# More gate projections by seven products, and stick-breaking attention started two blocks of input projection earlier, in another order of its blocks

## The chip, the cores and the metric

One Trainium2 chip, one of its cores. The metric is the device time of one execution of the whole program in microseconds (us), as the median of several executions.

## What is computed

Two transformer layers on 1024 positions of width 1024, all in float32. The first layer projects the normed input with `w_in` and feeds four branches (a short convolution, stick-breaking attention, an RWKV-7 recurrence, a gated spatial mix), weights each by its own sigmoid gate (4 x 1024 columns of the same projection), sums them, and ends in a feed-forward network. The second layer has two kinds of softmax attention. The parts that the change touches:

```
def short_conv_mixer(z, conv_w):
    b_gate, c_gate, xin = jnp.split(z, 3, axis=-1)
    return b_gate * causal_dwconv(c_gate * xin, conv_w)

def stick_breaking_attention(q, k, v):
    """A[t,s] = sig(z_ts) * prod_{s<j<t} (1 - sig(z_tj)), s < t."""
    ...
    def block(args):
        qi, bi = args
        z = jnp.einsum('bhqd,bhkd->bhqk', qi, kh).astype(jnp.float32) * scale
        mask = kpos[None, :] < qpos[:, None]
        log_beta = jax.nn.log_sigmoid(z)
        log_keep = jnp.where(mask, log_beta - z, 0.0)
        suffix = lax.cumsum(log_keep, axis=3, reverse=True) - log_keep
        attn = jnp.where(mask, jnp.exp(log_beta + suffix), 0.0)
        return jnp.einsum('bhqk,bhkd->bhqd', attn.astype(vh.dtype), vh)
...
gates = jax.nn.sigmoid((proj[..., GATE_OFF:] + gate_b)).reshape(bsz, t, N_BRANCH, D_MODEL)
merged = (gates[:, :, 0] * (y_a @ sc_out) + gates[:, :, 1] * (y_b @ sb_out)
          + gates[:, :, 2] * (y_c @ rw_out) + gates[:, :, 3] * (y_d @ sg_out))
```

## The kernel before

**Blocks.** The input projection is cut into blocks of 128 output columns by all 1024 positions. To keep float32 precision each operand is split into a high and a low part, and a product takes three matmuls (high by high, low by high, high by low). A block is 8 slices of the inner dimension x 2 halves of 512 positions x 3 = 48 matmuls of 128x512 (`whole`, L1244 to L1246, and `dense`, L1372 to L1374, which is the same in four quarters of 12). Results land in one of two places of PSUM, `gp[:, t % 2]`, where t is the block's number; whoever reads the block out adds one to `p_free0` or `p_free1`, and block t+2 waits for that. POOL splits the raw weights of each block (`split_weights`: a cast to `w_hi`, L954, and a subtraction to `w_lo`, L956). Which columns a block takes is given by the tuple `DENSE`.

**Order on TensorE.** Eight blocks (t = 0 to 7); then pairs of gate blocks (`gate_product`, L1403 to L1405), each pair by seven products of 12 matmuls in place of the eight that two plain blocks take; the sums between the products are DVE's (L2723 to L2735), the sigmoids ACT's. Then blocks t = 8 to 13 (v, q and k of the attention); then blocks 14 to 27 (`T_SB` = 14 to `T_RW` = 28) with the stick-breaking attention between their quarters; then the eight blocks of the recurrence, and all the rest.

**Stick-breaking attention in steps.** A *unit* m of the sixteen is one block of 128 queries (`qb`) for one pair of heads (`ft`); its scores are `w` = 128 (qb + 1) columns wide for each of the two heads. Before the change unit m is `qb, ft = divmod(m, 2)`. A *step* is one quarter of a block (12 matmuls) and then what `sb_pieces(step)` names, in this order: outputs, turns, scores.

- scores (PE, L1445), up to 512 columns a step, so units 8 to 15 need two steps; ACT makes both sigmoids from them (`sb_sig`, L2210; `sb_keep`, L2211);
- the cut of the diagonal (POOL `sb_cut`, L1001), once for the unit; in POOL's program it stands among the `split_weights` calls, which stand at `step % 4 == 2`;
- two running products (DVE scans, L2767), then the multiplication of `sb_sig` by them (L2772);
- turns (PE transposes, L1456), up to four tiles a step, each copied to `sb_pt` by ACT (L2227) before the next turn may write the same bank;
- outputs (PE, L1466) a step after their turn; when a unit's last one is done, ACT copies `y_b` (L2223), and the next unit's first output waits for that (`sb_y_free`).

Unit m starts its scores at step `SB_START[m]`. Its first turn is at step `SB_START[m + 1]`, and waits for DVE (`sb_p`); an engine takes its work in program order, so the matmuls behind that turn wait with it. There are 56 steps.

**Short convolution.** Blocks 14 to 17 are the convolution's output gate (columns 0, 1; ACT copies them to `y_a`) and its input gate (2, 3; ACT copies to `sc_c`); blocks 18 and 19 are its input. DVE reads these from PSUM in `short_conv` after units 8 and 9, and multiplies with `y_a` at its end (L2759). Blocks 20 to 27 are gates; ACT puts their sigmoids into `gate_late`, which lies where `sc_c` was, so it waits for `sc_done` first.

## Time and profile before

| | |
|---|---|
| median of 3 runs | 2448.02 us (2446.23 to 2448.09) |
| the profiled execution | 2444.71 us, span 2443.0 us |
| PE busy in the span | 2372.1 us (97%) |
| weight loads (PEld) | 1881.1 us (77%) |
| DVE, ACT, POOL busy | 1169.0 (48%), 769.2 (31%), 1112.4 us (46%) |
| DMA queue q1, share of 16 engines | 24.5% |
| blocks 14 to 27 with the attention between | 388.8 to 623.0 us of the span |

The span is the time from the profile's first to its last instruction, and the execution's own time is 1.7 us more. PE is busy nearly all the time, so what matters is how many matmuls it has, and the stretches in which it is idle. The profiled execution was 3.3 us below the median of the runs.

### The profile page before, as it was taken

How to read it: one execution, taken by the hardware profiler on the slowest of the kernel's cores; microseconds unless marked ns; L12 is line 12 of the kernel's file. 1: busy time of each engine (PE TensorE's matmuls, PEld its weight loads, DVE VectorE, ACT ScalarE, POOL GpSimd, SP SyncE). 2: the span in 40 equal slices, each digit the busy share in tenths (PEclk: the TensorE clock that was granted, in tenths of full speed). 3: DMA queues.
4: the chain of work that ended last, by engine and by line, in shares of the span. 5: the costliest groups of instructions: out<-in, count | busy, mean ns of one | idle time of the engine just before them, and what ended most of it. 6: DMA issues, size and time to landing. Idle time of an engine off the chain costs nothing.

```text
span 2443.0 us, 36336 instructions
## 1 busy us (share of the span) xinstructions
PE 2372.1 (97%) x15494; PEld 1881.1 (77%) x15494; DVE 1169.0 (48%) x1445; ACT 769.2 (31%) x1191; POOL 1112.4 (46%) x755
## 2 busy tenths in 40 slices
PE   7999999999999999999999999999999999999999
PEld 6888887666779868878888887888777886656677
DVE  7811101554195355676667775333443216755621
ACT  4233312333222121254434441011332006564511
POOL 4477733333234278577777773343732220013221
PEclk9999999999999999999999999999999999999999
DMA  5233321011200146422222225322213112000024
GB/s 198 79 104 104 104 77 43 27 52 59 63 27 13 38 155 207 138 69 90 83 87 78 78 95 190 104 86 69 52 43 104 49 37 63 13 12 24 2 64 126
DMA packets 208250, 189.83 MB, mean 78 GB/s; under 512 B 16714, under 2 KB 186929, under 8 KB 207834
## 3 DMA queue, kind: packets, MB, share of 16 engines
q1 hardware_dynamic: 208090, 187.51, 24.5%
q8 instruction: 123, 2.02, 0.3%
q14 instruction: 37, 0.30, 0.0%
HBM read 141.31 MB, written 45.13 MB: 76 GB/s over the span
## 4 chain that ended last, share of the span: by engine, by line
PE 81%; issue 7%; DVE 6%; POOL 5%; ACT 2%; DMA 0%; SPq 0%; POOLq 0%; DVEq 0%; ACTq 0%
PE gp L1244 8%; PE gp L1246 8%; PE gp L1245 8%; PE sm L1785 3%; PE sm L1786 3%; PE sm L1784 3%; PE gp L1784 3%; PE gp L1785 3%; PE gp L1786 3%; PE gp L1887 3%; PE gp L1903 2%; POOL w_lo L956 2%; PE sm L1813 2%; PE sm L1815 2%; PE sm L1814 2%
## 5 line engine op out<-in xcount | busy, mean ns | idle before, releaser
L954 POOL CAST w_hi<-w_raw 128x1024 fp32r<-128x1024 f32 (+1 forms) x101 | 110.1, 1090 | 730.8 <-PE gp L1246 364.4
L956 POOL TENSOR_TENSOR w_lo<-w_raw,w_hi 128x1024 fp32r<-128x1024 f32 (+1 forms) x109 | 295.8, 2713 | 8.7 <-ACT w_hi L2314 0.5
L1244 PE MATMUL gp<-h_hi,w_hi 128*128 128x512 f32 x704 | 282.5, 401 | 0.0
L1246 PE MATMUL gp<-h_hi,w_lo 128*128 128x512 f32 x704 | 274.3, 390 | 0.0
L1245 PE MATMUL gp<-h_lo,w_hi 128*128 128x512 f32 x704 | 273.9, 389 | 0.0
L1244 PEld LDWEIGHTS gp<-h_hi,w_hi 128*128 128x128 f32 x704 | 132.2, 188 | 33.1 <-issue 6.6
L1245 PEld LDWEIGHTS gp<-h_lo,w_hi 128*128 128x128 f32 x704 | 132.2, 188 | 31.0 <-issue 4.3
L1246 PEld LDWEIGHTS gp<-h_hi,w_lo 128*128 128x128 f32 x704 | 132.1, 188 | 28.0
L2767 DVE TENSOR_TENSOR_SCAN sb_run<-sb_keep,ones_row 128x128 f32<-128x128 f32 (+7 forms) x32 | 77.2, 2453 | 135.7 <-POOL sb_keep L1001 135.7
L1161 POOL TENSOR_TENSOR w_lo<-w_sum,w_hi 128x512 fp32r<-128x512 f32 x66 | 96.3, 1459 | 45.8 <-ACT w_hi L2373 45.8
L2534 ACT ACTIVATE att_s<-att_s,small 128x1024 f32<-128x1024 f32 (+7 forms) x128 | 99.0, 775 | 5.2 <-DVE small L3242 4.8
L1372 PE MATMUL gp<-h_hi,w_hi 128*128 128x512 f32 x240 | 99.3, 414 | 0.0
L1374 PE MATMUL gp<-h_hi,w_lo 128*128 128x512 f32 x240 | 93.9, 391 | 0.0
L1373 PE MATMUL gp<-h_lo,w_hi 128*128 128x512 f32 x240 | 93.8, 391 | 0.0
L2546 ACT COPY att_pt<-gp 128x512 f32<-128x512 f32 (+1 forms) x80 | 44.9, 562 | 120.3 <-PE gp L1887 120.3
L1887 PE MATMUL gp<-ident,att_s 128*128 128x128 f32 x576 | 77.5, 280 | 0.0
L2456 ACT CAST g_hi<-g_stage 128x1024 fp32r<-128x1024 f32 x22 | 23.1, 1054 | 168.2 <-DMA g_stage<-g_spill 123.7
L1784 PE MATMUL gp<-x_hi_T,w_hi 128*128 128x512 f32 x176 | 69.8, 396 | 5.9 <-DVE up_u L3086 5.2
L1113 POOL TENSOR_TENSOR merged<-merged,gated 128x1024 f32<-128x1024 f32 x24 | 64.8, 2700 | 17.8 <-DVE gated L2958 15.4
L1813 PE MATMUL gp<-g_hi,w_hi 128*128 128x512 f32 x176 | 69.2, 393 | 3.0 <-DVE g_lo L3131 3.0
L1887 PEld LDWEIGHTS gp<-ident,att_s 128*128 128x128 f32 x576 | 61.6, 141 | 12.0 <-issue 10.1
L1001 POOL TENSOR_SCALAR_AFFINE_SELECT sb_sig<-sb_sig 128x256 f32<-128x256 f32 x16 | 6.5, 408 | 140.2 <-ACT sb_keep L2211 140.2
(631 smaller groups left out, 6296.2 us busy)
## 6 DMA issues: line engine op xcount, KB each, us to landing
w_raw<-in_w_in SPq DMA_DIRECT2D x69, 512.0 KB, 4.0
gate_in<-gates_spill SPq DMA_DIRECT2D x30, 512.0 KB, 4.4
gates_spill<-gate_out SPq DMA_DIRECT2D x24, 512.0 KB, 5.9
w_raw<-in_w_up SPq DMA_DIRECT2D x22, 512.0 KB, 5.2
up_raw<-in_w_up SPq DMA_DIRECT2D x22, 512.0 KB, 5.1
g_spill<-hid SPq DMA_DIRECT2D x22, 512.0 KB, 2.6
g_stage<-g_spill SPq DMA_DIRECT2D x22, 512.0 KB, 4.3
w_raw<-in_w_down SPq DMA_DIRECT2D x22, 512.0 KB, 3.6
```

What stands on the lines that cost most here:

```text
L954: pool.tensor_copy(w_hi[:, t % 2, 0:n], w_raw[:, t % 2, 0:n]).then_inc(s["w_high"], 1)
L956: pool.tensor_tensor(w_lo[:, t % 2, 0:n], w_raw[:, t % 2, 0:n], w_hi[:, t % 2, 0:n].bitcast(F32), ALU.subtract).then_inc(s["w_split"], 1)
L1244: pe.matmul(o, wh, hi[:, k0 + k, c], start=(k == 0), stop=False)
L1245: pe.matmul(o, wh, lo[:, low[k] if low else k0 + k, c], start=False, stop=False)
L1246: mm = pe.matmul(o, wl, hi[:, k0 + k, c], start=False, stop=(k == n - 1))
L1372: pe.matmul(o, wh, h_hi[:, k, c], start=(k == 0), stop=False)
L1784: pe.matmul(o, wh, xh[:, :], start=(i < 4 and j == 0), stop=False, skip_group_check=True)
L1785: pe.matmul(o, wh, xl[:, :], start=False, stop=False, skip_group_check=True)
L1786: mm = pe.matmul(o, wl, xh[:, :], start=False, stop=(j == 3), skip_group_check=True)
L1813: pe.matmul(o, wh, hi[:, cols], start=(k == 0), stop=False)
L1887: mm = pe.transpose(bank(4 + r % 3)[:, P * n:P * n + P], s_buf[:, at_place(u), hh, P * k:P * k + P], ident[:, :])
L2534: act.activation(s_buf[:, at_place(u), hh, 0:w], s_buf[:, at_place(u), hh, 0:w], ACT.Exp, scale=-1.0, bias=at_small(0, u, hh), accum_out=a ...
```

## The change

Two more pairs of gate blocks are made by seven products (12 pairs in place of 10), and four fewer plain gate blocks (4 in place of 8) are left at the end of the attention's stretch. The plain blocks ahead of the attention are v, v, q0, k0; blocks 12 and 13 (q1, k1) now stand inside the attention's stretch, which is blocks 12 to 23: 12 blocks, 48 steps. So the attention begins at the fifth of the blocks behind the pairs. Units are taken in a new order, `SB_ROWS`: query blocks 0 to 3 of the first pair of heads, then 0 to 3 of the second, then as before. `SB_START` is closer, and a unit's first turn is at `SB_START[m + 1] + 1`, one step later than the next unit's first scores. Before the scores of unit 4, the first with q1 and k1, PE waits until both have been read out. The convolution's input gate is blocks 14 and 15, its input 16 and 17, its output gate 18 and 19: ACT copies the last no more, and DVE multiplies the block in PSUM with `sc_c` into `y_a` (`conv_gated`, after units 12 and 13). DVE's scans wait for `sb_p`, its own last multiplication.

```diff
 T_PAIRS = 8
-T_SB = 14
-T_RW = 28
+T_SB = 12
+T_RW = 24
...
-GATE_PAIRS = 10
-DENSE = (20, 22, 23, 21) + (24, 25, 26, 27) + (10, 11, 6, 7, 8, 9) + (0, 1, 2, 3, 4, 5) + tuple(range(48, 56))
-GATES = (0, 1, 2, 3) + tuple(4 + GATE_PAIRS * m + p for p in range(GATE_PAIRS) for m in (1, 0)) + tuple(range(24, 32))
+GATE_PAIRS = 12
+DENSE = (20, 22, 23, 21) + (24, 25, 26, 27) + (10, 11, 6, 8, 7, 9) + (2, 3, 4, 5, 0, 1) + tuple(range(52, 56))
+GATES = (0, 1, 2, 3) + tuple(4 + GATE_PAIRS * m + p for p in range(GATE_PAIRS) for m in (1, 0)) + tuple(range(28, 32))
 RW_ORDER = (6, 2, 0, 4, 3, 1, 5, 7)
 BRANCH_GATES = (0, 3, 1, 2)
-SB_START = tuple(2 + 2 * m for m in range(8)) + tuple(18 + 4 * m for m in range(9))
+SB_ROWS = ((0, 0), (1, 0), (2, 0), (3, 0), (0, 1), (1, 1), (2, 1), (3, 1)) + tuple((n // 2, n % 2) for n in range(8, 16))
+SB_START = (0, 2, 4, 6, 8, 9, 10, 12, 14, 17, 20, 23, 26, 30, 34, 38, 42)
...
             starts = [(m, step - SB_START[m]) for m in range(PAIRS)]
-            turns = [(m, step - SB_START[m + 1]) for m in range(PAIRS)]
-            return ([(m, c - 1) for m, c in turns if 1 <= c <= m // 4 + 1],
-                    [(m, c) for m, c in turns if 0 <= c <= m // 4],
-                    [(m, c) for m, c in starts if 0 <= c <= m // 8])
+            turns = [(m, step - SB_START[m + 1] - 1) for m in range(PAIRS)]
+            return ([(m, c - 1) for m, c in turns if 1 <= c <= sb_turns(m)],
+                    [(m, c) for m, c in turns if 0 <= c < sb_turns(m)],
+                    [(m, c) for m, c in starts if 0 <= c < sb_parts(m)])
...
                         for z in range(2):
                             pe.wait_ge(s[f"p_free{z}"], frees_before(T_SB + z))
+                    elif (m, c) == (4, 0):
+                        for z in range(2):
+                            pe.wait_ge(s[f"p_free{z}"], frees_before(T_SB + 2 + z))
                     sb_scores(m, c)
...
                 n = DENSE[t]
-                if n in (4, 5):
+                if n < 2 or n in (4, 5):
...
-                elif n < 2:
-                    act.copy(y_a[:, n, :], ps).then_inc(done, 1)
...
-                for z in range(2):
-                    dve.wait_ge(s[f"p_free{z}"], frees_before(T_SB + 4 + z))
+                dve.wait_ge(s[f"p_free{n}"], frees_before(t))
...
-                ins = dve.tensor_tensor(y_a[:, n, :], y_a[:, n, :], acc, ALU.mult)
+
+            def conv_gated(n):
+
+                t = T_SB + 6 + n
+                dve.wait_ge(s["p_ready"], t + 1)
+                dve.tensor_tensor(y_a[:, n, :], gp[:, t % 2, :], sc_c[:, n, :], ALU.mult).then_inc(s[f"p_free{t % 2}"], 1)
                 if n == 1:
-                    ins.then_inc(s["sc_done"], 1)
+                    for z in range(2):
+                        dve.wait_ge(s[f"p_free{z}"], frees_before(t) + 1)
+                    dve.tensor_copy(small[:, 8:9], ones[:, 0:1]).then_inc(s["sc_done"], 1)
 
             for m in range(PAIRS):
-                w = P * (m // 2 + 1)
+                w = P * (SB_ROWS[m][0] + 1)
                 wait("sb_cut")
+                if m:
+                    dve.wait_ge(s["sb_p"], m)
...
-                if m in (8, 9):
-                    short_conv(m - 8)
+                if m in (9, 10):
+                    short_conv(m - 9)
+                elif m in (12, 13):
+                    conv_gated(m - 12)
```

What this does to the order of instructions is read from the two programs. "waits" names the semaphores that an instruction waits for.

On POOL, around the cuts of the units 9 to 11 in the program after (`L1010` is the cut, `L963` and `L965` the split of a block's weights; these rows begin with the cut of unit 9):

```order
L1010 AFFINE_SELECT sb_sig<-sb_sig 128x2x128 [waits sb_e]
L1010 AFFINE_SELECT sb_keep<-sb_keep 128x2x128
L1010 AFFINE_SELECT sb_sig<-sb_sig 128x2x128 [waits sb_e]
L1010 AFFINE_SELECT sb_keep<-sb_keep 128x2x128
L963 CAST w_hi<-w_raw 128x1024 [waits p_ready,w_loaded0]
L965 TENSOR_TENSOR w_lo<-w_raw,w_hi 128x1024 [waits w_high]
L1010 AFFINE_SELECT sb_sig<-sb_sig 128x2x128 [waits sb_e]
L1010 AFFINE_SELECT sb_keep<-sb_keep 128x2x128
L963 CAST w_hi<-w_raw 128x1024 [waits p_ready,w_loaded1]
L965 TENSOR_TENSOR w_lo<-w_raw,w_hi 128x1024 [waits w_high]
```

Before, from unit 8 on, each unit's cut was followed by a split; the rows begin with the cut of unit 8 (`L1001`, splits `L954` and `L956`):

```order
L1001 AFFINE_SELECT sb_sig<-sb_sig 128x2x128 [waits sb_e]
L1001 AFFINE_SELECT sb_keep<-sb_keep 128x2x128
L954 CAST w_hi<-w_raw 128x1024 [waits p_ready,w_loaded0]
L956 TENSOR_TENSOR w_lo<-w_raw,w_hi 128x1024 [waits w_high]
L1001 AFFINE_SELECT sb_sig<-sb_sig 128x2x128 [waits sb_e]
L1001 AFFINE_SELECT sb_keep<-sb_keep 128x2x128
```

The cuts of units 9 and 10 now stand together, with no split between them, and the split behind the cut of unit 10 is that of block 18.

On PE, the whole of step 10's attention work in the program after (`L1475` an output, `L1465` a turn, `L1454` scores, then the next quarter's first matmul):

```order
L1475 MATMUL sm<-sb_pt,v_sb 64x128 [waits sb_pt_copied,sb_y_free]
L1475 MATMUL sm<-sb_pt,v_sb 64x128 x3
L1465 MATMUL sm<-ident,sb_sig 128x128 [waits sb_pt_copied]
L1465 MATMUL sm<-ident,sb_sig 128x128 x3
L1465 MATMUL sm<-ident,sb_sig 128x128 [waits sb_pt_copied,sb_p]
L1465 MATMUL sm<-ident,sb_sig 128x128
L1454 MATMUL sm<-k_sb,q_sb 128x384 [waits sb_e] x2
L1381 MATMUL gp<-h_hi,w_hi 128x512
```

No step before had two turns, each with its own wait for ACT's copy; here unit 3's second turn and unit 4's first stand one behind the other.

On DVE, from the scans of unit 12 to the first of unit 14 after the change (`L2786` a scan, `L2791` the multiplication, `L2774` `conv_gated`):

```order
L2786 SCALAR_TENSOR_TENSOR sb_run<-sb_keep,ones_row 128x896 [waits sb_p,sb_cut]
L2786 SCALAR_TENSOR_TENSOR sb_run<-sb_keep,ones_row 128x896
L2791 TENSOR_TENSOR sb_sig<-sb_sig,sb_run 128x2x895 [waits sb_run]
L2774 TENSOR_TENSOR y_a<-gp,sc_c 128x1024 [waits p_ready]
L2786 SCALAR_TENSOR_TENSOR sb_run<-sb_keep,ones_row 128x896 [waits sb_p,sb_cut]
L2786 SCALAR_TENSOR_TENSOR sb_run<-sb_keep,ones_row 128x896
L2791 TENSOR_TENSOR sb_sig<-sb_sig,sb_run 128x2x895 [waits sb_run]
L2774 TENSOR_TENSOR y_a<-gp,sc_c 128x1024 [waits p_ready]
L2778 COPY small<-ones 128x1 [waits p_free1,p_free0]
L2786 SCALAR_TENSOR_TENSOR sb_run<-sb_keep,ones_row 128x1024 [waits sb_p,sb_cut]
```

Before, the two blocks of the output gate were read out by ACT at once, and DVE's part of it was the last row of each `short_conv`, behind units 8 and 9:

```order
L2756 SCALAR_TENSOR_TENSOR sc_c<-sc_cx,col,sc_c 128x1023 [waits dve_own]
L2756 SCALAR_TENSOR_TENSOR sc_c<-sc_cx,col,sc_c 128x1022 [waits dve_own]
L2759 TENSOR_TENSOR y_a<-y_a,sc_c 128x1024 [waits dve_own]
L2767 SCALAR_TENSOR_TENSOR sb_run<-sb_keep,ones_row 128x640 [waits sb_cut]
L2767 SCALAR_TENSOR_TENSOR sb_run<-sb_keep,ones_row 128x640
L2772 TENSOR_TENSOR sb_sig<-sb_sig,sb_run 128x2x639 [waits sb_run]
```

The read-out of blocks 18 and 19 now stands on DVE behind the scans of units 12 and 13.

## Rows read from the trace of the kernel before

**Rows 1.** Busy time by stretch: us; busy us and instructions of each engine; granted clock.

```profile
388.80:623.00 234.20, 224.66 (x1202) 159.19 (x1201) 110.35 (x59) 77.63 (x164) 72.93 (x60) 1.00 0.15 46
623.00:800.00 177.00, 167.19 (x2727) 141.48 (x2727) 102.43 (x94) 47.21 (x51) 63.10 (x33) 0.99 0.13 38
...
730.00:740.00 10.00, 9.38 (x300) 9.15 (x302) 5.88 (x7) 2.19 (x3) 4.69 (x2) 0.83 0.01 3
```

**Rows 2.** Waits from 388 to 624: who waited for whom, us, times, longest.

```profile
PEld sm L1456 <- DVE sb_sig L2772: 12.7, 10, 2.4
...
PE sm L1456 <- DVE sb_sig L2772: 9.5, 8, 2.2
```

**Rows 3.** Timeline of ACT, read-out of two plain blocks: start, duration, [idle before].

```profile
378.01 1.02 ACT L2132 COPY k_sb<-gp 128x1024 f32<-128x1024 f32 x1 [9.85 <-PE gp L1246]
388.89 1.02 ACT L2132 COPY k_sb<-gp 128x1024 f32<-128x1024 f32 x1 [9.86 <-PE gp L1246]
```

**Rows 4.** Timeline of DVE, the same sum in two pairs of gate blocks.

```profile
158.69 0.69 DVE L2723 TENSOR_TENSOR ones_row<-ones_row,sm 128x512 f32<-128x512 f32 x1 [7.52 <-PE sm L1405]
...
177.73 0.69 DVE L2723 TENSOR_TENSOR ones_row<-ones_row,gp 128x512 f32<-128x512 f32 x1 [7.52 <-PE gp L1405]
```

**Rows 5.** Timeline of PE, unit 15 from last scores to first turn.

```profile
590.40 1.13 PE L1445 MATMUL sm<-k_sb,q_sb 64*128 64x512 f32 x4
...
594.40 0.66 PE L1466 MATMUL sm<-sb_pt,v_sb 128*64 128x128 f32 x8
...
598.34 0.66 PE L1466 MATMUL sm<-sb_pt,v_sb 128*64 128x128 f32 x8
...
602.28 0.66 PE L1466 MATMUL sm<-sb_pt,v_sb 128*64 128x128 f32 x8
604.30 0.66 PE L1456 MATMUL sm<-ident,sb_sig 128*128 128x128 f32 x4 [1.36 <-DVE sb_sig L2772]
```

**Rows 6.** Timeline of ACT, first sigmoid of those scores.

```profile
591.56 0.60 ACT L2210 ACTIVATE sb_sig<-sm 128x512 f32<-128x512 f32 x1 [0.47 <-PE sm L1445]
```

**Rows 7.** Timeline of POOL: cut of unit 15, split behind it, a later undisturbed split.

```profile
593.70 0.41 POOL L1001 TENSOR_SCALAR_AFFINE_SELECT sb_sig<-sb_sig 128x256 f32<-128x256 f32 x1 [13.61 <-ACT sb_keep L2211]
...
594.41 1.04 POOL L954 CAST w_hi<-w_raw 128x1024 fp32r<-128x1024 f32 x1
595.54 4.24 POOL L956 TENSOR_TENSOR w_lo<-w_raw,w_hi 128x1024 fp32r<-128x1024 f32 x1
...
608.97 2.40 POOL L956 TENSOR_TENSOR w_lo<-w_raw,w_hi 128x1024 fp32r<-128x1024 f32 x1
```

**Rows 8.** Timeline of DVE: scans of units 6, 7 and 15, multiplication of unit 15.

```profile
447.86 2.34 DVE L2767 TENSOR_TENSOR_SCAN sb_run<-sb_keep,ones_row 128x512 f32<-128x512 f32 x2 [4.80 <-POOL sb_keep L1001]
...
456.53 5.30 DVE L2767 TENSOR_TENSOR_SCAN sb_run<-sb_keep,ones_row 128x512 f32<-128x512 f32 x2 [5.07 <-POOL sb_keep L1001]
...
594.50 7.42 DVE L2767 TENSOR_TENSOR_SCAN sb_run<-sb_keep,ones_row 128x1024 f32<-128x1024 f32 x2 [9.94 <-POOL sb_keep L1001]
601.95 2.29 DVE L2772 TENSOR_TENSOR sb_sig<-sb_sig,sb_run 128x2046 f32<-128x2046 f32 x1
```

**Rows 9.** Timeline of PE and DVE: last scores, next output, multiplication of unit 9 (640 columns).

```profile
484.37 0.49 PE L1445 MATMUL sm<-k_sb,q_sb 64*128 64x128 f32 x4
...
487.74 0.66 PE L1466 MATMUL sm<-sb_pt,v_sb 128*64 128x128 f32 x8
...
492.50 1.49 DVE L2772 TENSOR_TENSOR sb_sig<-sb_sig,sb_run 128x1278 f32<-128x1278 f32 x1
```

**Rows 10.** Timeline of PE and ACT: an output and its copy, a turn and its copy.

```profile
441.31 0.44 PE L1466 MATMUL sm<-sb_pt,v_sb 128*64 128x128 f32 x4
443.11 0.66 PE L1456 MATMUL sm<-ident,sb_sig 128*128 128x128 f32 x4 [1.36 <-DVE sb_sig L2772]
...
441.80 0.27 ACT L2223 COPY y_b<-sm 128x128 f32<-128x128 f32 x1 [2.76 <-PE sm L1466]
443.81 0.59 ACT L2227 COPY sb_pt<-sm 128x512 f32<-128x512 f32 x1 [1.74 <-PE sm L1456]
```

More of the change, by code:

```diff
@@ L56 @@
 T_PAIRS = 8
-T_SB = 14
-T_RW = 28
-T_BR = 36
-T_WO = 44
-T_FFN = 52
+T_SB = 12
+T_RW = 24
+T_BR = 32
+T_WO = 40
+T_FFN = 48
 T_IN2 = T_FFN + FT
@@ L66 @@
 T_END = T_OUT + 8
-P_RW = 28
-P_BR = 36
+P_RW = 24
+P_BR = 32
 P_WO = P_BR + 32
@@ L579, in hybrid_layers, with sb_turns, sb_parts @@
         PAIRS = 2 * NB
+        def sb_turns(m):
+            return SB_ROWS[m][0] // 2 + 1
+        def sb_parts(m):
+            return SB_ROWS[m][0] // 4 + 1
         def sb_chunks(m):
-            before = sum(n // 4 + 1 for n in range(m))
-            return [(c, before + c) for c in range(m // 4 + 1)]
+            before = sum(sb_turns(n) for n in range(m))
+            return [(c, before + c) for c in range(sb_turns(m))]
         def sb_blocks(m, c):
-            return [2 * k + hh for k in range(2 * c, min(2 * c + 2, m // 2 + 1)) for hh in range(2)]
+            return [2 * k + hh for k in range(2 * c, min(2 * c + 2, SB_ROWS[m][0] + 1)) for hh in range(2)]
         def sb_pieces(step):
             starts = [(m, step - SB_START[m]) for m in range(PAIRS)]
-            turns = [(m, step - SB_START[m + 1]) for m in range(PAIRS)]
-            return ([(m, c - 1) for m, c in turns if 1 <= c <= m // 4 + 1],
-                    [(m, c) for m, c in turns if 0 <= c <= m // 4],
-                    [(m, c) for m, c in starts if 0 <= c <= m // 8])
+            turns = [(m, step - SB_START[m + 1] - 1) for m in range(PAIRS)]
+            return ([(m, c - 1) for m, c in turns if 1 <= c <= sb_turns(m)],
+                    [(m, c) for m, c in turns if 0 <= c < sb_turns(m)],
+                    [(m, c) for m, c in starts if 0 <= c < sb_parts(m)])
         def sb_scores_through(m, c):
-            return sum(2 * (n // 8 + 1) for n in range(m)) + 2 * (c + 1)
+            return sum(2 * sb_parts(n) for n in range(m)) + 2 * (c + 1)
         def at_unit(u):
@@ L754, in _ @@
                 load_weights(t + 2)
-                if t >= T_SB + 6:
-                    store_dense(t, t + 4, gate_late)
+                if t >= T_SB + 8:
+                    store_dense(t, t + 8, gate_late)
             for t in range(T_RW + 2, T_BR + 2):
@@ L996, in sb_cut @@
             def sb_cut(m):
-                pool.wait_ge(s["sb_e"], sb_scores_through(m, m // 8))
-                qb = m // 2
+                pool.wait_ge(s["sb_e"], sb_scores_through(m, sb_parts(m) - 1))
+                qb = SB_ROWS[m][0]
                 for buf, fill in ((sb_sig[:, m % 2], 0.0), (sb_keep, 1.0)):
@@ L1049, in _ @@
                     for m, c in sb_pieces(step)[2]:
-                        if c == m // 8:
+                        if c == sb_parts(m) - 1:
                             sb_cut(m)
@@ L1437, in sb_scores @@
             def sb_scores(m, c):
-                qb, ft = divmod(m, 2)
+                qb, ft = SB_ROWS[m]
                 w = P * (qb + 1)
@@ L1459, in sb_output @@
             def sb_output(m, c, r):
-                qb, ft = divmod(m, 2)
+                qb, ft = SB_ROWS[m]
                 if c == 0 and m:
@@ L1467, in sb_output @@
                                    sb_pt[:, b, :], start=(k == 0), stop=(k == qb), skip_group_check=True)
-                if c == m // 4:
+                if c == sb_turns(m) - 1:
                     mm.then_inc(s["sb_y"], 1)
@@ L2114, in dense_out @@
                 if n >= 24:
-                    q = t - 4 if t < T_PAIRS else t + 4
+                    q = t - 4 if t < T_PAIRS else t + 8
                     if q >= 2:
@@ L2202, in sb_sigmoids @@
             def sb_sigmoids(m, c):
-                w = min(HALF, P * (m // 2 + 1) - HALF * c)
+                w = min(HALF, P * (SB_ROWS[m][0] + 1) - HALF * c)
                 if c == 0 and m:
@@ L2215, in _ @@
                 if step % 4 == 3:
-                    if step == 4 * 6 + 3:
+                    if T_SB + step // 4 == T_SB + 8:
                         act.wait_ge(s["sc_done"], 1)
@@ L2220, in _ @@
                 for m, c in outputs:
-                    if c == m // 4:
+                    if c == sb_turns(m) - 1:
                         wait("sb_y")
-                        act.copy(y_b[:, m % 2, P * (m // 2):P * (m // 2) + P], sm[:, 3, 0:P]).then_inc(s["sb_y_free"], 1)
+                        qb, ft = SB_ROWS[m]
+                        act.copy(y_b[:, ft, P * qb:P * qb + P], sm[:, 3, 0:P]).then_inc(s["sb_y_free"], 1)
                 for m, c in turns:
```

## Prediction

> **What bounds the kernel now.** Read first, in the profile's page, the busy shares: TensorE is busy 97% of the span, so only two things can move the time, the number of matmul slots and the stretches in which PE is idle. Then the busy time by stretch. Blocks 14 to 27 with the attention between take 234.2 us of which PE is busy 224.7 [rows 1]; the reader is to see that 9.5 us are idle, in a stretch where DVE is busy only 110 us and ACT and POOL less than 80. No engine is full there, so something is late rather than too much. The waits of the stretch say what: all of PE's 9.5 us, 8 times, are turns that wait for DVE's multiplication; the weight-load queue in front of the same turns shows 12.7 us, 10 times [rows 2]. The timelines then give the chain from a unit's last scores to its first turn.
>
> **A matmul slot.** Two plain blocks in a row are read out 10.88 us apart [rows 3], for 48 matmuls, so a quarter is 2.72 us and a matmul 0.227. The same sum in two successive gate pairs is 19.04 us apart [rows 4], for 84 matmuls: again 0.227, so the pairs run without a gap.
>
> **Term 1, the pairs.** Two pairs more cost 2 x 19.04 = 38.08 us of PE; four plain blocks less give 4 x 10.88 = 43.52. The difference is 5.44 us, 24 matmuls. It lies on the path, since PE is the path in both stages. What the pairs add on ACT, DVE and POOL lies beside PE, which has not waited for them in the ten pairs there were; the four blocks' splits and stores are gone. The attention's own work on PE is the same 40 turns, 40 outputs and 24 pieces of scores, only in another order, so it costs nothing more. ACT's two copies to `y_a` and the last row of DVE's `short_conv` are replaced by one DVE multiplication each; all of this lies beside PE.
>
> **Term 2, the turns that wait.** Take unit 15. From its last scores on PE to the first turn that could start is 604.30 - 590.40 = 13.9 us [rows 5]: 1.16 to the first sigmoid [rows 6], 2.1 for four sigmoids, 0.8 for the cut [rows 7], 7.42 for two scans and 2.29 for the multiplication [rows 8]. What PE has to do in that time, its *cover*, is counted in steps. Scores and a quarter are 594.40 - 590.40 = 4.00, so 1.28 for scores of 512 columns; a step of output, turn and quarter is 3.94 [rows 5], so 1.22 for output and turn together and 0.6 for one of them. Before, `SB_START[15]` is 46, so the last scores are at step 47 and the turn at step 50: 1.28 + 3 x 2.72 + 2 x 1.22 + 0.6 = 12.5 us against 13.9. The missing 1.4 us is the wait that the row shows, 1.36. This arithmetic can now be done for the new numbers.
>
> After, the last scores of unit 15 are at step 39 and its turn at step 43: 1.28 + 4 x 2.72 + 3 x 1.22 + 0.6 = 16.4 us against the same 13.9, as one more quarter and one more output and turn lie between. That is 2.5 us to spare. Units 12 to 14 have the same four quarters, and the next unit's first scores too, so 3 or more. Narrower units have shorter chains. Unit 9 (640 columns) took 493.99 - 484.37 = 9.6 us, and its last scores (128 columns) 487.74 - 484.37 - 2.72 = 0.65 of PE [rows 9]. After, unit 8 has 3 quarters: 0.65 + 8.16 + 1.22 + 0.6 + 1.28 = 11.9 us, 2.3 to spare. For 768 columns I interpolate between 9.6 and 13.9: 11.1. The cover of units 10 and 11 is 12.8 and 13.2 (last scores 0.85, 3 quarters, one or two steps of output and turn, scores of the next unit, an output): 1.7 and 2.1 to spare. For 512 columns, four widths of 128 less than 1024 at 0.8 each (scans 0.53: (7.42 - 5.30) / 4; multiplication 0.27), the chain is 10.7 [rows 8]; unit 7 has 12.7 of cover, 2.0 to spare. Units 0 to 6 come out at 2 or more. So no turn waits for DVE; before, ten did.
>
> What was lost: PE's idle time says 9.5, the load queue 12.7 [rows 2]. A matmul's record (0.39 on the page) is longer than its slot (0.227), so a wait behind a quarter hides 0.16 or more of itself; half of them stand there. I take 10.5, with 9.5 and 12.7 as ends.
>
> **What makes a chain longer.** A scan that meets a split is slower: two scans of 512 columns took 2.34 us alone and 5.30 beside the split that stands behind the cut of unit 7, 2.96 more [rows 8]; the split's subtraction took 4.24 in place of 2.40 [rows 7]. The chain of 13.9 has this in it. In the new order of POOL, splits stand behind the cuts of units 0, 2, 5, 7, 8 and 10 to 15, behind 11 units in place of 12, and I have counted every chain above with it.
>
> The other side of it is the split itself. That of block 18 now stands behind the cut of unit 10, late, as the block starts two quarters further on. From unit 10's last scores: 3.0 to the end of the cut, 4.8 for a split beside two scans of 768 (1.13 and 3.7, between 2.40 and 4.24), 7.8 in all; the cover is 0.85 + 2 x 2.72 + 1.22 + 2.3 = 9.8. It costs nothing, with 2 us to spare. The Trainium skill (SBUF — State Buffer, section "Who interferes with whom") says that VectorE and GpSimd share a port pair under an exclusive lock, and that the loser waits out the winner's whole instruction. That the trace agrees is seen in the two rows of scans: they are slowed, and so is the split. By that rule the subtraction could lose both scans of 768, 1.7 us each, in place of the 1.3 that the rows give it; block 18 would start 0.1 us late, and the sum below would be 14.0 in place of 14.1.
>
> **Term 3, a new wait.** In step 10 unit 3's second turn and unit 4's first stand together, and the second waits for ACT's copy of the first out of the same bank. A copy starts 0.70 us after its turn's start and takes 0.59 [rows 10], together 1.3 less the turn's own 0.6 and a little for the signal: 0.8. In step 11 unit 4's first output waits for the copy of `y_b` of unit 3; alone that would be 0.49 + 0.27 after the output's start [rows 10], less the output's 0.6, so 0.2 to 0.4, but in this step ACT first reads out block 14 (1.02 [rows 3]), so 1.0. Sum 1.8, ends 1.0 and 3.0 (if ACT comes late to both). Queued behind these waits are PE's scores of unit 6 and turn of unit 5, whose chains have over 3 us to spare.
>
> **Costs of nothing.** DVE's wait for `sb_p` is for its own work, done long before the next cut arrives (DVE idle 5 to 10 us before each pair of scans [rows 8]); without that cover it would be some 0.1 us each. `conv_gated` frees blocks 18 and 19 behind units 12 and 13: by the chains that is 12.4 us after the end of step 27 (31), while the blocks that want the place start at step 32 (36), 4 quarters and the attention between, 15 to 16 us; more than 2 us to spare. The wait before unit 4's scores is for a copy of 1.02 us behind a quarter of 2.72. Behind the attention all engines stand to PE as before: DVE is done with its last unit 18 us ahead of the recurrence, as against 19.
>
> **Sum.** 5.4 + 10.5 - 1.8 = 14.1 us. Against the profiled execution: 2444.7 - 14.1 = 2430.6 us. That execution was 3.3 under the median of its runs, so against the median 2448.0 - 14.1 = 2434 us, which I forecast (0.6% faster). The ends of the terms give 5.4 + 9.5 - 3.0 = 12 and 5.4 + 12.7 - 1.0 = 17: 2431 to 2436, and with 1 us for the median itself 2430 to 2437 (0.75).
>
> **Rivals.**
> *The waits move instead of going* (0.13). For it: six units have only 1.7 to 2.5 us to spare, and a chain's length comes from two engines that slow each other, as the same pair of scans takes 2.34 or 5.30. If splits meet the multiplications too, or ACT comes 1 us late to its sigmoids, chains grow by 2 to 3 us, and six to eight turns wait 0.5 to 1 each. Against it: every chain is already counted with the split in it. It gives back 4 to 8 us: 2438 to 2442.
> *Only the pairs count* (0.06). The turns wait as before, for instance because two units' work in closer steps makes ACT late everywhere: a gain of 5.4 at most, and less if some waits grow: 2442.6 to 2448. Against it: ACT is busy 78 of 234 us [rows 1].
> *Slower* (0.03). Place: blocks 20 and 21, whose PSUM place is freed by DVE behind the scans of units 12 and 13, and block 22 behind the gates that wait for `sc_done`. If a scan stands 3 us later than counted, PE loses 0.5 us; to end above 2453, 14 + 5 us must be lost, so DVE would have to be some 12 us late at both blocks, one whole chain. Nothing in the rows does that; the price is about 2455.
> *More gain* (0.03): 2426 to 2430, if the recurrence's stretch, in which PE is idle 10 of 177 us [rows 1], loses a fall of the clock. There the granted clock was 0.83 from 730 to 740 us, 1.2 GHz for part of that time, behind waits of PE, and worth up to 1.7 us; a shift in time can take such a fall away or add one. The Trainium skill (TensorE: Matmul & The Clock Gate, section "What's actually happening") has the slow clock as the default that activity releases; by that, fewer waits in the attention can only help, and the trace agrees in that 1.00 was granted there in spite of the waits.
>
> **How the numbers follow.** A measurement of this kernel tells about 0.2%, 4.9 us, from no change. The forecast, the moved waits and more gain are faster by over that: 0.75 + 0.13 + 0.03 = 0.91; only the pairs is within it for the most part, 0.06; slower 0.03. The range holds the likeliest case and half of the moved waits: 2429.5 to 2440.
>
> **What would show it.** In the profile after: two DVE pair sums still 19.04 apart, twelve times; the stretch of blocks 12 to 23 about 203.5 us (234.2 - 21.8 - 10.5 + 1.8 = 203.7); among its waits, turns waiting for DVE gone, and two of about 1 us for ACT's copies; scans of unit 9 without the 2.96 us, of units 10 to 15 with it. The prediction is wrong if turns still wait for DVE by more than 3 us together, if blocks 18, 20 or 21 start with a wait for `w_lo` or for DVE, or if the stretches behind 623 us change their length by more than 2 us.

## The result, and the profile after

| | median | range | |
|---|---|---|---|
| before | 2448.06 us | 2446.23 to 2452.20, 4 runs | |
| after | 2432.85 us | 2428.84 to 2435.85, 4 runs | 0.9934 [0.9915, 0.9954] |
| after, measured again | 2430.83 us | 2427.37 to 2434.29, 5 runs; before beside it 2448.84, 9 runs | 0.9929 [0.9917, 0.9942] |

The changed kernel is 15.2 us faster, in the second measurement 18.0. Forecast were 14.1 us and 2434, with a range of 2430 to 2437 in which both medians lie, so the prediction was right. The profiled execution after took 2435.85 us, its span 2433.8, 9.2 us less than the span of before. Why this is less than the medians say is told below.

The busy time of the kernel after, in the stretch from the last read-out of a plain block ahead of the attention to the last gate block of the attention's stretch (us; busy us and instructions of PE, PEld, the weight-load queue, DVE, ACT, POOL; granted clock, DMA share, GB/s):

```profile
407.50:608.40 200.90, 199.45 (x1098) 140.85 (x1098) 107.19 (x60) 72.19 (x159) 64.91 (x56) 1.00 0.13 37
```

Beside [rows 1]: 200.9 us in place of 234.2, and PE is idle for 1.45 of them in place of 9.5. The reader is to see that the idle time is gone while DVE, ACT and POOL do about the same work as before (107, 72 and 65 us against 110, 78 and 73). The prediction had 203.7 here; where the other 2.8 us are is told in the account below. Where the edges of that stretch lie is read in the timeline of ACT after (start, duration, idle before):

```profile
407.50 1.02 ACT L2142 COPY k_sb<-gp 128x1024 f32<-128x1024 f32 x1 [11.63 <-PE gp L1255]
...
453.06 1.01 ACT L2138 COPY sc_c<-gp 128x1024 f32<-128x1024 f32 x1 [1.09 <-PE gp L1383]
453.96 0.27 ACT L2234 COPY y_b<-sm 128x128 f32<-128x128 f32 x1
...
608.43 1.12 ACT L2130 ACTIVATE gate_late<-gp,col 128x1024 f32<-128x1024 f32 x1 [2.18 <-PE gp L1383]
...
620.16 1.12 ACT L2245 ACTIVATE zr<-gp,small 128x1024 f32<-128x1024 f32 x1 [10.46 <-PE gp L1255]
```

The two read-outs at 407.50 and 608.43 are its edges, and the row at 620.16 is the first block of the recurrence. The waits of the kernel after between 380 and 650 us (who for whom, us, times, longest) hold two of PE in this stretch:

```profile
PE sm L1465 <- ACT sb_pt L2238: 0.8, 1, 0.8
PE sm L1475 <- ACT y_b L2234: 0.7, 1, 0.7
```

Not one turn waits for DVE, where there were ten [rows 2]. The two waits are those of term 3. The timeline of PE after shows both in place, the second turn of step 10 and the first output of step 11:

```profile
447.40 0.66 PE L1465 MATMUL sm<-ident,sb_sig 128*128 128x128 f32 x4
448.82 0.41 PE L1465 MATMUL sm<-ident,sb_sig 128*128 128x128 f32 x2 [0.77 <-ACT sb_pt L2238]
...
452.95 0.66 PE L1475 MATMUL sm<-sb_pt,v_sb 128*64 128x128 f32 x8
454.29 0.44 PE L1475 MATMUL sm<-sb_pt,v_sb 128*64 128x128 f32 x4 [0.68 <-ACT y_b L2234]
```

The first is 0.77 (forecast 0.8). The second is 0.68 (forecast 1.0): as foreseen, ACT first reads out a block (453.06 for 1.01) and only then copies `y_b` (453.96), both in the ACT rows above.

The pairs: in the timeline of DVE after, the sum that was 19.04 us apart in two successive pairs [rows 4] still is, in the last two of twelve:

```profile
332.33 0.69 DVE L2734 TENSOR_TENSOR ones_row<-ones_row,gp 128x512 f32<-128x512 f32 x1 [7.52 <-PE gp L1414]
...
351.37 0.69 DVE L2734 TENSOR_TENSOR ones_row<-ones_row,sm 128x512 f32<-128x512 f32 x1 [7.52 <-PE sm L1414]
```

**The chains.** Last scores and turn of unit 15 in PE's timeline after, and the scans and multiplication behind them in DVE's (the row at 486.33 is the scans of unit 9):

```profile
576.74 1.13 PE L1454 MATMUL sm<-k_sb,q_sb 64*128 64x512 f32 x4
...
593.15 0.66 PE L1465 MATMUL sm<-ident,sb_sig 128*128 128x128 f32 x4
```

```profile
486.33 2.88 DVE L2786 TENSOR_TENSOR_SCAN sb_run<-sb_keep,ones_row 128x640 f32<-128x640 f32 x2 [4.87 <-POOL sb_keep L1010]
...
580.84 7.42 DVE L2786 TENSOR_TENSOR_SCAN sb_run<-sb_keep,ones_row 128x1024 f32<-128x1024 f32 x2 [8.06 <-POOL sb_keep L1010]
588.29 2.29 DVE L2791 TENSOR_TENSOR sb_sig<-sb_sig,sb_run 128x2046 f32<-128x2046 f32 x1
```

Unit 15's chain is as long as before: its multiplication ends at 590.58, 13.84 us after the scores began. What changed is the cover. The turn stands at 593.15, 16.41 us after the scores, so it has 2.57 us to spare (forecast 2.5). Units 8, 7, 10 and 11 have 2.08, 1.86, 1.86 and 2.29 (forecast 2.3, 2.0, 1.7, 2.1). The scans of unit 9, with no split behind its cut any more, take 2.88; those of unit 15, with one, 7.42 as before [rows 8].

**A measure that leaves the rest out.** Falls of the granted clock come and go elsewhere in the program. So the kernels are compared below by one stretch of their profiled executions, from the first sum that DVE makes for the first gate pair (139.66 us before, 141.95 after) to the read-out of the first block of the recurrence (634.02 and 620.16). It holds all pairs, all plain blocks behind them and the attention. Before it is 494.4 us, after 478.2: 16.1 less. In a second profile of each it was 494.4 and 478.2 again.

### The profile page after: what moved, and what is told of

Its sections match the earlier page's. It is cut to its first block, busy times and chain, and to the rows that moved or that the text cites. A ratio compares the mean times of both kernels' runs of the same rounds, so it can differ in the third digit from the quotient of the medians.

```text
span 2433.8 us, 36368 instructions
## 1 busy us (share of the span) xinstructions
PE 2369.4 (97%) x15470; PEld 1879.2 (77%) x15470; DVE 1175.6 (48%) x1456; ACT 774.1 (32%) x1205; POOL 1124.2 (46%) x769
## 4 chain that ended last, share of the span: by engine, by line
PE 88%; DVE 5%; POOL 3%; ACT 2%; issue 1%; DMA 1%; SPq 0%; POOLq 0%; DVEq 0%; ACTq 0%
PE gp L1253 8%; PE gp L1255 8%; PE gp L1254 8%; PE sm L1797 3%; PE sm L1796 3%; PE sm L1798 3%; PE gp L1796 3%; PE gp L1797 3%; PE gp L1798 3%; PE gp L1899 3%; PE gp L1915 2%; PE gp L1381 2%; PE gp L1383 2%; PE gp L1382 2%; PE sm L1412 2%; PE gp L1412 2%
## 5 line engine op out<-in xcount | busy, mean ns | idle before, releaser
L963 POOL CAST w_hi<-w_raw 128x1024 fp32r<-128x1024 f32 (+1 forms) x97 | 106.1, 1094 | 711.1 <-PE gp L1255 341.7
L965 POOL TENSOR_TENSOR w_lo<-w_raw,w_hi 128x1024 fp32r<-128x1024 f32 (+1 forms) x105 | 284.8, 2712 | 8.3 <-ACT w_hi L2325 0.5
L1253 PE MATMUL gp<-h_hi,w_hi 128*128 128x512 f32 x672 | 270.9, 403 | 0.0
L1255 PE MATMUL gp<-h_hi,w_lo 128*128 128x512 f32 x672 | 262.4, 390 | 0.0
L1254 PE MATMUL gp<-h_lo,w_hi 128*128 128x512 f32 x672 | 262.3, 390 | 0.0
L1253 PEld LDWEIGHTS gp<-h_hi,w_hi 128*128 128x128 f32 x672 | 126.5, 188 | 32.2 <-issue 6.8
L1254 PEld LDWEIGHTS gp<-h_lo,w_hi 128*128 128x128 f32 x672 | 126.6, 188 | 29.7 <-issue 4.3
L1255 PEld LDWEIGHTS gp<-h_hi,w_lo 128*128 128x128 f32 x672 | 126.5, 188 | 27.0
L2786 DVE TENSOR_TENSOR_SCAN sb_run<-sb_keep,ones_row 128x128 f32<-128x128 f32 (+7 forms) x32 | 74.1, 2355 | 84.8 <-POOL sb_keep L1010 84.8
L1381 PE MATMUL gp<-h_hi,w_hi 128*128 128x512 f32 x208 | 86.1, 414 | 0.0
L1383 PE MATMUL gp<-h_hi,w_lo 128*128 128x512 f32 x208 | 81.5, 392 | 0.0
L1382 PE MATMUL gp<-h_lo,w_hi 128*128 128x512 f32 x208 | 81.1, 390 | 0.0
L1899 PEld LDWEIGHTS gp<-ident,att_s 128*128 128x128 f32 x576 | 61.9, 142 | 12.3 <-issue 10.5
L1170 POOL TENSOR_TENSOR w_lo<-w_raw,w_hi 128x512 fp32r<-128x512 f32 x44 | 58.3, 1325 | 25.7 <-ACT w_hi L2384 25.7
```

Source lines behind the costliest of these rows:

```text
L965: pool.tensor_tensor(w_lo[:, t % 2, 0:n], w_raw[:, t % 2, 0:n], w_hi[:, t % 2, 0:n].bitcast(F32), ALU.subtract).then_inc(s["w_split"], 1)
L1170: pool.tensor_tensor(lo, w_quad(n), hi.bitcast(F32), ALU.subtract).then_inc(s["up_low"], 1)
L1253: pe.matmul(o, wh, hi[:, k0 + k, c], start=(k == 0), stop=False)
L1254: pe.matmul(o, wh, lo[:, low[k] if low else k0 + k, c], start=False, stop=False)
L1255: mm = pe.matmul(o, wl, hi[:, k0 + k, c], start=False, stop=(k == n - 1))
L1381: pe.matmul(o, wh, h_hi[:, k, c], start=(k == 0), stop=False)
```

## Experiments

Each has a median of 4 or 5 runs, and beside it the kernel before on the same chip: 2448.84 us (9 runs) for the first four here, 2448.82 (9 runs) for the next three, 2448.38 (7 runs) for two more.

| kernel | median, us | ratio to before | stretch, us |
|---|---|---|---|
| after, measured again | 2430.83 | 0.9929 [0.9917, 0.9942] | 478.2 |
| after with ten pairs | 2436.56 | 0.9953 [0.9941, 0.9966] | 483.7 |
| before, turns one step later | 2434.30 | 0.9937 [0.9923, 0.9951] | 482.1 |
| before, splits behind the scans | 2437.08 | 0.9953 [0.9940, 0.9965] | 483.6 |
| after, turns one step earlier | 2463.42 | 1.0061 [1.0048, 1.0075] | 512.2 |
| after, no step with two turns | 2430.27 | 0.9922 [0.9909, 0.9936] | 476.8 |
| after, output gate copied by ACT | 2431.17 | 0.9927 [0.9915, 0.9940] | 478.3 |
| turns earlier, splits behind the scans | 2432.44 | 0.9935 [0.9920, 0.9950] | 482.9 |
| turns later, splits behind the scans | 2433.20 | 0.9942 [0.9925, 0.9958] | 482.1 |

### The kernel after, once more

No edit. 

> The kernel after, unchanged, on the same chip as the runs beside it. 12 to 17 us faster than before; its profile has 5.4 us of gain up to the attention and 10.7 in the stretch of the attention, and what is more or less than 16 in the whole is the number of falls of the granted clock elsewhere.

It gained 18.0 us where the first measurement said 15.2, and its stretch was 478.2. The stretch repeats to 0.1 us, the median of the whole program does not to 2 us.

### Term 1 alone: ten pairs in the new order

```diff
-GATE_PAIRS = 12
+GATE_PAIRS = 10
-T_RW = 24
+T_RW = 28
```

The four blocks come back as plain gates behind the attention's 48 steps. 

> The new schedule of the attention alone: everything as after the change, but ten pairs of gate blocks and eight plain gate blocks, of which four stand behind the attention's steps. Theory (two terms that add): the schedule gives what the stretch showed, 10.7 us less of PE there, and the pairs give 5.4, so this kernel is at before minus 10 to 11 us, 5.4 above the kernel after. In the profile the two waits for ACT's copies are there and no turn waits for DVE. Rival (the terms are not independent: fewer blocks to hide the chains is what brings the stretch's gain): other than 4 to 7 us above the kernel after.

The stretch is 483.7, 5.4 us longer than after, and the median 5.7 longer. So two pairs in place of four plain blocks are worth 5.4 us, the 24 matmuls that the prediction counted, and the new order without them is worth 10.7.

### Term 2 alone: the turn one step later

```diff
 # the kernel before
-            turns = [(m, step - SB_START[m + 1]) for m in range(PAIRS)]
+            turns = [(m, step - SB_START[m + 1] - 1) for m in range(PAIRS)]
...
+                if m:
+                    dve.wait_ge(s["sb_p"], m)
```

One quarter more of cover, in the old order of units with 56 steps and ten pairs. 

> The kernel before with one thing changed: a unit's first turn stands one step behind the next unit's first scores in place of the same step (and DVE waits for its own multiplication before a scan). Theory (the turns stand too near): one step more of cover, 2.7 to 3.9 us, is more than the longest wait of 2.2, so all ten waits go and the stretch from block 14 to the recurrence is 10.5 us shorter, the kernel 10 to 11 us faster than before. Rival (the new order of the units and the closer steps do it, by fewer changes between projection and attention work): 4 us faster or less.

No turn waits for DVE, and the stretch is 482.1, 12.3 us less than before. That is 1.8 more than the 10.5 of the prediction, and only 3.8 short of the whole change.

### Term 2 from its other side: a shorter chain

```diff
 # the kernel before, POOL's program
                     if step % 4 == 2:
+                        if cuts:
+                            pool.wait_ge(s["sb_p"], cuts)
                         split_weights(t + 1)
```

The steps stay as they were. Each split in the attention's stretch waits until DVE is done with the unit cut before it. 

> The kernel before with one thing changed: in the attention's stretch POOL splits a block's weights only when DVE has finished the unit that was cut last. Theory (DVE's scans are lengthened by 2.96 us by the split beside them): scans of units 7 to 15 fall to 2.3 to 4.5 us for two, every turn's multiplication ends 3 us earlier, all waits of up to 2.2 us go, 10.5 us faster than before. Rival (the split's overlap only moves the port's time elsewhere, for example into the multiplications, or blocks start late because the splits are later): waits for w_lo at block starts, 3 us faster or less.

The scans of unit 15 in the timeline of DVE of this kernel:

```profile
585.77 4.47 DVE L2771 TENSOR_TENSOR_SCAN sb_run<-sb_keep,ones_row 128x1024 f32<-128x1024 f32 x2 [10.99 <-POOL sb_keep L1001]
```

4.47 us for two scans of 1024 that took 7.42 beside a split [rows 8]: 2.95 less, as much as two scans of 512 had lost (5.30 - 2.34). Why the loss does not hang on the width is seen when the two scans of unit 15 in the kernel before are shown one by one (two windows of DVE's timeline):

```profile
594.50 3.10 DVE L2767 TENSOR_TENSOR_SCAN sb_run<-sb_keep,ones_row 128x1024 f32<-128x1024 f32 x1 [9.94 <-POOL sb_keep L1001]
...
597.52 4.40 DVE L2767 TENSOR_TENSOR_SCAN sb_run<-sb_keep,ones_row 128x1024 f32<-128x1024 f32 x1
```

Beside [rows 7] they read as DVE and POOL taking turns, a whole instruction at a time. The first scan, 2.29 us with no split beside it, stands beside the cast (594.41 for 1.04) and takes 0.81 more. The subtraction starts at 595.54 but ends at 599.77, 2.17 after that scan (597.60), about the 2.40 that it takes alone. The second scan, 2.27 alone, ends 2.15 after the subtraction. So two scans lose most of a cast and of a subtraction, 2.95 us together, at either width, and the subtraction loses what is left of the first scan: 1.84 beside 1024 columns, but 0.78 beside the 512 of unit 7 (3.18 in place of 2.40).

All turns come in time, and the stretch is 483.6, 10.7 us less than before. That is what the waits alone had cost, since neither the steps nor the covers changed: inside the prediction's ends of 9.5 and 12.7, and 0.2 from the 10.5 that it took.

**Where the other 1.6 us of the later turn are.** Both experiments remove all waits for DVE, and one gains 1.6 us more. The table of waits has it, on the weight-load queue, as time with nothing to wait for. With the splits behind the scans (as in the kernel before), and then with the turns one step later (us, times, longest):

```profile
PEld gp L1376 <- issue: 14.3, 30, 0.8
```

```profile
PEld gp L1372 <- issue: 12.8, 21, 0.8
```

In a step that ends on an output, with no turn or scores behind it, the first weight load of the next quarter comes some 0.17 us late (1.5 us over nine gaps). The matmuls show the same: the next quarter's first one starts 0.20 us after the last output's start, but 0.03 after the last turn's, in every such step of every kernel here that ran it at full clock. Ten steps ended so before, two with the later turns, one in the kernel after, where the row of waits says 12.6 us in 20. Eight steps less are 1.4 of the 1.6 us here, and nine less in the kernel after are 1.5, which no term of the prediction had.

### The cover taken away: turns one step earlier

```diff
 # the kernel after
-            turns = [(m, step - SB_START[m + 1] - 1) for m in range(PAIRS)]
+            turns = [(m, step - SB_START[m + 1]) for m in range(PAIRS)]
```

> The kernel after with one thing taken back: a unit's first turn stands at the same step as the next unit's first scores again. Theory (cover against chain): margins of 1.7 to 2.5 us less one step of 2.7 to 3.9 us; by the same arithmetic units 5, 7, 8, 10 and 11 wait 2.6 to 3.4 us, units 2 and 12 to 15 wait 0.7 to 2.2, together 22 us more than after, so slower than before by 4 to 10 us. Rival (the closer steps alone bring the gain, the turn's place is of no account): within 4 us of the kernel after.

It is 14.6 us slower than before, where 4 to 10 had been expected: 2463.42 us, and the stretch is 33.9 us longer than after. The table of waits of this kernel has the waits for DVE that were expected:

```profile
PE sm L1465 <- DVE sb_sig L2791: 21.2, 11, 3.3
```

With two waits for ACT of 0.8 and 0.4, PE waits 22.4 us, 21 more than in the kernel after, of the 34. Most of the rest is the clock. Three of the eleven turns in PE's timeline:

```profile
454.67 0.85 PE L1465 MATMUL sm<-ident,sb_sig 128*128 128x128 f32 x4 [2.80 <-DVE sb_sig L2791]
...
524.03 1.11 PE L1465 MATMUL sm<-ident,sb_sig 128*128 128x128 f32 x4 [3.30 <-DVE sb_sig L2791]
...
601.36 0.77 PE L1465 MATMUL sm<-ident,sb_sig 128*128 128x128 f32 x4 [1.81 <-DVE sb_sig L2791]
```

The granted clock of four windows of 10 us of the same kernel is the number after PE's, DVE's, ACT's and POOL's busy times:

```profile
430.00:440.00 10.00, 8.16 (x42) 5.66 (x42) 5.13 (x5) 3.98 (x7) 0.77 (x2) 1.00 0.19 54
450.00:460.00 10.00, 6.83 (x33) 4.08 (x32) 4.87 (x4) 2.76 (x7) 4.03 (x4) 0.83 0.18 52
520.00:530.00 10.00, 6.70 (x21) 3.76 (x20) 8.39 (x6) 2.92 (x6) 0.57 (x1) 0.66 0.18 52
600.00:610.00 10.00, 8.64 (x37) 4.87 (x38) 1.30 (x1) 4.49 (x8) 0.00 (x0) 0.83 0.04 16
```

The window from 430 has its wait too (PE is busy 8.16 of 10) and keeps 1.00. The windows from 450, 520 and 600, behind waits of 2.80, 3.30 and 1.81 us, were granted 0.83, 0.66 and 0.83. A turn that takes 0.66 us at full clock took 0.85 and 1.11 there. Three more such windows stand behind waits of 2.58, 2.67 and 2.87 us. 0.83 over 10 us means that about a third of them were at the 1.2 GHz level, in which PE did half of what it does at 2.4 GHz: 1.7 us lost for each, an estimate from these rows. Seven such thirds, the window from 520 counted twice, are 12 us. Five more steps than in the kernel after end on an output, 0.17 each. With the 21 of waits that makes up all but 0.2 of the 33.9.

### The same turns, a shorter chain

The edit of the turn one step earlier and the wait of the splits together, on the kernel after. 

> The kernel after with turns one step earlier (as in the run that took that back alone, 32 us slower than after in the median and 33.9 in the profile's stretch), and POOL's splits waiting for DVE's last unit. Theory (the loss is chains of which 2.96 us are the split beside the scans; turns then wait 0.5 us or less, one block's start 1.7 for its late split; with short waits the clock does not fall): stretch from block 12 to the recurrence within 4 us of that of the kernel after, granted clock 1.00 in it. Rival (an early turn costs 30 us for another reason, or the falls of the clock do not hang on the waits): 15 us or more slower than after, or clock falls in the stretch in spite of short waits.

The stretch falls from 512.2 to 482.9 and the median by 31 us, to 2432.44. So nearly the whole cost of the early turn came from the length of the chain. What is left over the kernel after is 4.7 us, where up to 4 had been expected. PE's waits in it:

```profile
PE gp L1385 <- POOL w_lo L965: 1.8, 1, 1.8
...
PE sm L1469 <- DVE sb_sig L2795: 0.4, 1, 0.4
```

The chains fit but for 0.4 us, and block 18 waits 1.8 us for `w_lo`, since its split now comes after the scans. This is the edge at which the prediction had 2 us to spare. Behind that wait the granted clock fell once more, to 0.86 from 510 to 520 us, which had not been expected.

### Both cures on the old order

The turn one step later and the wait of the splits together, on the kernel before. 

> The kernel before with both single changes, turns one step later and splits behind the scans. Either alone took every wait for DVE out of PE's row, 12.3 and 10.7 us of the stretch. Theory (the waits were worth 10.5 to 11, the other 1.6 of the later turns are issue gaps of 0.17 us where an output alone is followed by a quarter, ten such steps against two): with both, 12.3 again and no more. Rival (short waits remain in one of them and add up): 13.5 us or more.

The stretch is 482.1, as with the later turn alone and as expected. Once nothing waits, a shorter chain gives nothing more. The prediction's model, a chain against its cover, holds here too.

### Term 3: no step with two turns

```diff
 # the kernel after
-SB_START = (0, 2, 4, 6, 8, 9, 10, 12, 14, 17, 20, 23, 26, 30, 34, 38, 42)
+SB_START = (0, 2, 4, 6, 8, 10, 11, 12, 14, 17, 20, 23, 26, 30, 34, 38, 42)
```

> The kernel after with SB_START of units 5 and 6 one step later (10 and 11), so that no step has two turns and no output of one unit stands beside the last output of another. Theory: the two waits of 0.77 and 0.68 us for ACT's copies go and nothing comes in their place, the stretch is 1.4 to 1.8 us shorter; in the whole 1 to 2 us less than after, which the median may not tell. Rival: the waits move to units 5 to 7, whose scores are now later, and the stretch is as long or longer.

PE does not wait at all in the attention, and the stretch is 476.8, 1.4 us less than after. That is the 0.77 and the 0.68. The median is 2430.27 us, the lowest of all kernels here, but 1.4 us are less than the medians can tell.

### The output gate from PSUM or by way of ACT

```diff
 # the kernel after
+                elif n < 2:
+                    act.copy(y_a[:, n, :], ps).then_inc(done, 1)
...
-                dve.tensor_tensor(y_a[:, n, :], gp[:, t % 2, :], sc_c[:, n, :], ALU.mult).then_inc(s[f"p_free{t % 2}"], 1)
+                ins = dve.tensor_tensor(y_a[:, n, :], y_a[:, n, :], sc_c[:, n, :], ALU.mult)
```

> The kernel after with ACT copying the convolution's output gate to y_a again, and DVE multiplying the copy behind units 12 and 13. Theory (the gate from PSUM is worth nothing in time): same as after within 1 us in the attention's stretch. Rival (DVE's read-out behind the scans holds PSUM places, or ACT's copy makes a sigmoid late): blocks 20 or 21 start 1 us or more earlier or later than after.

The stretch is 478.3 us against 478.2. Who reads the block out changes nothing, as PE waits for neither.

### The kernel before, profiled twice more

No edit, one execution each. 

> The kernel before, unchanged, for a second profile. All variants gained 1 to 2 us more in their medians than in their stretch up to the recurrence. Theory (waits of about 2 us bring a fall of the granted clock in some executions): this profile shows one or more falls in the attention's stretch, which is then 1.7 us longer for each than 494.3 us from the second product sum of the pairs to the first block of the recurrence. Rival (the further gain lies elsewhere): the stretch is 494.3 again, clock 1.00 in it.

> As the look before it: the same stretch of the unchanged kernel before, 494.3 us and clock 1.00 by the rival, longer by 1.7 for each fall by the theory.

The stretch was 494.4 and 497.5. The first repeats the profile of before, with 1.00 in the attention's stretch, as the rival had it. In the second PE has the same waits, but two of them were followed by a lower clock. Four windows of the second one:

```profile
450.00:460.00 10.00, 10.00 (x55) 6.97 (x54) 4.90 (x4) 3.50 (x7) 3.52 (x4) 1.00 0.01 2
460.00:470.00 10.00, 7.84 (x35) 5.06 (x34) 3.71 (x2) 2.92 (x6) 1.41 (x1) 0.83 0.18 52
580.00:590.00 10.00, 8.20 (x42) 5.26 (x41) 6.68 (x3) 2.29 (x6) 2.24 (x1) 0.91 0.00 1
590.00:600.00 10.00, 10.00 (x54) 6.95 (x53) 1.80 (x1) 5.36 (x10) 2.52 (x4) 0.92 0.35 105
```

In the first profile of before all four had 1.00 [rows 1], with the same waits of 2.2 and 1.8 us. So those waits sometimes bring a fall with them, which costs 3.1 us here. That the waits bring them about is read from what stands before them and from the turns one step earlier; what decides whether a wait of 2 us is followed by one stays open.

## Why the prediction was right

**Term 1, 5.44 us.** Right: 5.4 in the stretch.

**Term 2, 10.5 us.** The mechanism is right, shown from both sides, by a longer cover and by a shorter chain. The waits alone were worth 10.7. The arithmetic of the cover was right too: 16.4 for unit 15, 12.8 and 13.2 for units 10 and 11, and 16.41, 12.85 and 13.29 in the trace. The new order also takes away 1.5 us of late weight loads, which no term had. Two runs show these by their difference; that the gap belongs to an output at a step's end is read from the rows of all the kernels and was not tried by itself.

**Term 3, 1.8 us.** Two waits, both where they were put, 1.45 together: the turn 0.77 for 0.8, the output 0.68 for 1.0.

**The account** is then 5.4 + 10.7 + 1.5 - 1.45 = 16.15, against 16.1 measured in the stretch. The sum of 14.1 was 2.0 short, of which 1.5 is the missing term; it is small enough to lie in the range all the same. The stretch of blocks 12 to 23, forecast at 203.7 and measured at 200.9, has these 2.0 us and 0.85 of its edge: behind the last gate's last quarter an output now comes ahead of the recurrence, so the read-out of that gate stands 11.73 us before the next one and not 10.88.

**Costs of nothing.** `conv_gated`, the wait for `sb_p`, and the splits' new places cost nothing: PE has only two waits in the stretch, and with the output gate copied by ACT the time is the same. How near the edge block 18 stands is seen where its split comes after the scans. Its subtraction took 3.73 us (501.15 in POOL's timeline after), so it lost 1.33 beside the scans of 768, as the rows had given it. The other estimate of the prediction, that it could lose both scans at 1.7 each, did not come: as in unit 15, it waits for the rest of the first scan only, and the second scan waits for it.

**The rivals.** "Only the pairs count" is out, since the kernel with ten pairs gained 10.7 us in the stretch. The waits did not move. Their condition was real, though: a chain against a margin of 1.9 to 2.6 us. One step less of cover costs 34 us. The prediction's slower rival (2455, 21 us more than the forecast) had another place and no fall of the clock behind its waits, and did not occur either. The fall on which more gain was built, from 730 to 740 us, is still there after, 14 us earlier (0.85 from 710 to 720).

**Where the step behind 623 us failed.** The prediction said that the later stretches would keep their length within 2 us. In the profiled execution after they did not. Up to 710 us of the span it is 13.9 ahead of before, at its end only 9.2. Of the 16.1, 2.3 are lost ahead of the stretch (0.6 in the first 32 us, 1.7 in a fall of the clock to 0.83 from 60 to 70 us), and 4.7 behind 710 us. Three windows of the profile after, two from the recurrence's end and the merge, one from the second layer:

```profile
840.00:850.00 10.00, 9.74 (x25) 5.48 (x26) 3.67 (x3) 3.17 (x5) 6.30 (x5) 0.83 0.00 0
870.00:880.00 10.00, 7.33 (x24) 5.28 (x23) 3.58 (x3) 1.04 (x1) 7.40 (x4) 0.83 0.41 154
2010.00:2020.00 10.00, 9.16 (x44) 4.92 (x44) 5.36 (x17) 5.27 (x14) 0.00 (x0) 0.66 0.22 90
```

At the places that correspond to the first two, 14 us later, before has 1.00 throughout, and in the second layer one window at 0.83. Before has one fall that after has not, 0.86 from 800 to 810 us, so there the kernel after gains a little. From the first block of the recurrence to the end, before took 1809.0 us, in its two further profiles 1810.1 and 1810.7, and after 1813.6, 1813.9 when repeated. Over all kernels here it was 1807.7 to 1814.1, though they are the same program from there on but for the place of the gate blocks in memory. What decides these falls stays open. So does whether the new kernel is more prone to them: two with its order, the one with the output gate copied (1810.9) and the one with the turns earlier and the splits behind the scans (1807.7), were about as short as before, and two with the old order, with the turns later and with the splits behind the scans, took 1812.5 and 1812.6. Each fall moves the time of one execution by some 1.7 us.

The medians' 15.2 and 18.0 us fit the local 16.1 with this noise on it. The profiled execution of before was also 3 to 4 us under the medians of its kernel, and its third profile shows one way in which that comes about, a fall or two of the clock in the attention. How often it happens there was not measured.

What was gained is a matter of steps. The later turn alone takes 12.3 of the 16.1 us in the old order. The new order of units and the early start show no gain of their own: with ten pairs they give 10.7, later turn included. They fit the attention into 48 steps with the later turn in it, so that two more pairs can be made.

## What to carry to other kernels

Where a busy engine waits in turns for a chain on the others, compare the chain's length with the work that stands in its cover, unit by unit. One quarter of a block more, by moving the consumer one step, was worth 12.3 of the 16.1 us that the whole change gained, and keeping two slow helpers apart was worth 10.7. Measure such a change by a stretch whose edges lie outside of it but near, in each profile, since the end of the program carries several us of other things. And leave a margin: the step from 2 us to spare to 2 or 3 us late cost 34 us for 21 us of waits, because the clock fell behind them.

## What the runs showed of the hardware that was not expected

- TensorE's granted clock fell behind single waits of PE of 2.6 to 3.3 us, five of five in one kernel. Behind waits of 1.8 to 2.2 us it fell in some executions and not in others of the same program. In the kernel with 22 us of waits this cost some 12 us more, an estimate from its windows.
- Two scans on VectorE beside a cast and a subtraction on POOL took turns with them, a whole instruction at a time. The scans lost 2.95 us together whether they were 512 or 1024 columns wide (2.34 to 5.30, 4.47 to 7.42), most of the cast's 1.04 and the subtraction's 2.40; the subtraction of 2.40 took 3.18, 3.73 and 4.24 beside 512, 768 and 1024 columns.
- The weight load of a quarter that came straight behind an output, with no turn or scores between, was 0.17 us late with nothing to wait for (its first matmul 0.20 us after the last output's start, against 0.03 behind a turn): 1.5 us over nine steps.
